# The last stage of a fused decoder kernel: rows padded to the full height, a product moved to GpSimd, gathers issued one after another

## The reference

```
y = _moe(h, ...)                 # out.at[token].add(expert_row * weight): two expert rows per token
x = _layer_norm(ALPHA * x + gate2 * y, ln_g, ln_b)
# layer_norm: (x - mean) * rsqrt(var + EPS) * g + b, over the 1024 columns
```

## Time and profile before

| | us |
|---|---|
| median of 3 runs | 2516.42 |
| lowest and highest | 2508.06, 2516.82 |
| the profiled execution | 2516.12 |
| its span, first to last instruction | 2514.5 |
| the last stage in it | about 2445 to 2514.5 |

### The profile page before, as it was taken

The page is one execution under the profiler, slowest core; times in us unless marked ns, Lnnn a source line. Parts: engine busy times, 40 slices in busy tenths (PEclk is TensorE's granted clock), DMA queues, the critical chain, the costliest instruction groups (busy, mean ns, idle before and its releaser), DMA issues. The chain is left out here.

```text
span 2514.5 us, 39237 instructions
## 1 busy us (share of the span) xinstructions
PE 2263.1 (90%) x11454; PEld 1662.9 (66%) x11454; DVE 1380.7 (55%) x2350; ACT 1075.2 (43%) x1830; POOL 307.8 (12%) x387
## 2 busy tenths in 40 slices
PE   7999997869769999999698999999989399999976
PEld 4766665648558888887486665656667288888851
DVE  4223213658866755764583344433369767755657
ACT  3211213631136645654343343444331256754645
POOL 0000002640001101010110333000000011000102
PEclk8999997979879999999899999999989699999985
DMA  7566555643248867784745644232350378866956
GB/s 276 177 214 218 204 200 154 183 163 134 71 175 295 318 224 266 284 289 154 228 154 198 195 143 151 92 96 93 101 210 35 131 282 320 318 240 220 321 198 214
DMA packets 194483, 499.26 MB, mean 199 GB/s; under 512 B 19344, under 2 KB 39281, under 8 KB 187888
## 3 DMA queue, kind: packets, MB, share of 16 engines
q1 hardware_dynamic: 164910, 403.86, 46.9%
q0 software_dynamic: 18416, 64.11, 7.2%
q10 hardware_dynamic: 11058, 30.06, 3.2%
HBM read 432.41 MB, written 68.70 MB: 199 GB/s over the span
## 5 line engine op out<-in xcount | busy, mean ns | idle before, releaser
L2024 DVE TENSOR_TENSOR e_wl<-e_raw,e_wh 128x1024 fp32r<-128x1024 f32 x384 | 451.6, 1220 | 107.9 <-ACT e_wh L1936 107.5
L1936 ACT CAST e_wh<-e_raw 128x1024 fp32r<-128x1024 f32 x384 | 379.3, 1047 | 75.8 <-DMA e_raw<-in_e_gate 22.5
L1855 PE MATMUL e_psG<-e_wh,e_xh 128*128 128x512 f32 x784 | 322.0, 411 | 10.5 <-issue 7.7
L1857 PE MATMUL e_psG<-e_wh,e_xl 128*128 128x512 f32 x784 | 312.4, 398 | 0.0
L1856 PE MATMUL e_psG<-e_wl,e_xh 128*128 128x512 f32 x784 | 310.9, 397 | 0.0
L1855 PEld LDWEIGHTS e_psG<-e_wh,e_xh 128*128 128x128 f32 x784 | 149.1, 190 | 43.2 <-issue 8.7
L1857 PEld LDWEIGHTS e_psG<-e_wh,e_xl 128*128 128x128 f32 x784 | 148.7, 190 | 37.1
L1856 PEld LDWEIGHTS e_psG<-e_wl,e_xh 128*128 128x128 f32 x784 | 149.5, 191 | 32.0
L608 PE MATMUL in_ps<-in_w_upper,in_h_upper 128*128 128x512 f32 x384 | 155.7, 405 | 3.8 <-DVE in_h_lower L328 3.4
L1855 PE MATMUL e_psY<-e_wh,e_hh 128*128 128x512 f32 x392 | 155.3, 396 | 2.8 <-DVE e_hl L2047 2.8
L1857 PE MATMUL e_psY<-e_wh,e_hl 128*128 128x512 f32 x392 | 157.1, 401 | 0.0
(11 more groups left out here) (589 smaller groups left out, 4236.7 us busy)
## 6 DMA issues: line engine op xcount, KB each, us to landing
e_raw<-in_e_gate SPq DMA_DIRECT2D x32, 2048.0 KB, 11.9
e_raw<-in_e_up SPq DMA_DIRECT2D x32, 2048.0 KB, 9.2
e_raw<-in_e_down SPq DMA_DIRECT2D x32, 2048.0 KB, 8.2
x<-in_ada_w SPq DMA_DIRECT2D x40, 1024.0 KB, 5.3
yrows<-e_y ACTq DMA_DIRECT2D x49, 512.0 KB, 7.5
x<-in_cache SPq DMA_DIRECT2D x64, 320.0 KB, 3.3
a_pages<-in_cache SPq DMA_DIRECT2D x64, 320.0 KB, 3.5
qkvo<-in_out SPq DMA_DIRECT2D x48, 256.0 KB
```

The source lines that it names most:

```text
L1855: T.matmul(out, upper[:, k, :], wh[:, z, cols], start=k == 0, stop=False)
L1857: mm = T.matmul(out, lower[:, k, :], wh[:, z, cols], start=False, stop=k == PIECES * n - 1)
L1936: S.copy(wh[:, z, c * PC:(c + 1) * PC], raw[:, z, c * PC:(c + 1) * PC]).then_inc(s_hi[z], 1)
L2024: V.tensor_tensor(wl[:, z, at], raw[:, z, at], wh[:, z, at].bitcast(F32), ALU.subtract).then_inc(s_lo[z], 1)
```

## The change

Three edits, all in `stage_combine`:

1. The ones matrix, the two shift rows and their source have 128 rows instead of 33; the added rows are zeros in the shift rows.
2. `gated(t)` runs on GpSimd. It waits for `both(t)` and counts up a new semaphore `s_gated`, for which `residual(t)` waits. On VectorE `both(1)` now comes after `residual(0)`.
3. GpSimd issues tile 0's gathers, waits until they have landed, issues tile 1's, does `gated(0)`, waits until tile 1's have landed, and issues those of tiles 2, 3 and 4. Then it does `gated(t)` for t from 1 on, each followed by the gathers of tile t + 4.

```diff
-        lb33, both_rows, ones = sb("lb33", [33, D]), sb("lb_rows", [33, D], F32R), sb("ones33", [33, P], F32R)
+        lb33, both_rows, ones = sb("lb33", [P, D]), sb("lb_rows", [P, D], F32R), sb("ones_copy", [P, P], F32R)
+        s_gated = sem("gated")
...
-            for t in range(RING):
+            def gated(t):
+                n, z = rows_of(t), zr[0:rows_of(t), t % RING, :]
+                if t == PT:
+                    po.wait_ge(s_gateS, 16 * BATCHES)
+                elif t == 0:
+                    po.wait_ge(s_gate, 16)
+                nc.gpsimd.tensor_tensor(z, z, gate[0:n, t // PT, :], ALU.mult).then_inc(s_gated, 1)
+
+            gather(0)
+            po.wait_ge(s_g[0], 32)
+            gather(1)
+            po.wait_ge(s_both, 1)
+            gated(0)
+            po.wait_ge(s_g[1], 32)
+            for t in range(2, RING + 1):
                 gather(t)
-            for t in range(RING, TILES):
-                po.wait_ge(s_both, t - RING + 1)
-                gather(t)
+            for t in range(1, TILES):
+                po.wait_ge(s_both, t + 1)
+                gated(t)
+                if t + RING < TILES:
+                    gather(t + RING)
...
-            S.copy(ones[:], g.ones[0:33, :])
+            S.copy(ones[:], g.ones[:])
...
-            def gated(t):
-                n, z = rows_of(t), zr[0:rows_of(t), t % RING, :]
-                if t == PT:
-                    v.wait_ge(s_gateS, 16 * BATCHES)
-                else:
-                    v.wait_ge(s_gate, 16)
-                v.drain()
-                V.tensor_tensor(z, z, gate[0:n, t // PT, :], ALU.mult)
-
             def residual(t):
                 n, par, z = rows_of(t), t % 2, zr[0:rows_of(t), t % RING, :]
-                v.drain()
+                v.wait_ge(s_gated, t + 1)
                 V.scalar_tensor_tensor(out=z, in0=g.x[0:n, t, :], scalar=ALPHA, in1=z, op0=ALU.mult, op1=ALU.add,
                                        accum_out=total[0:n, par:par + 1])
...
             both(0)
-            gated(0)
-            both(1)
             for t in range(TILES):
                 residual(t)
-                if t + 1 < TILES:
-                    gated(t + 1)
                 if t == 0:
+                    both(1)
                     v.wait_ge(s_lg, 16)
                 centred(t)
                 reciprocal(t)
```

## The result

| | before | after |
|---|---|---|
| median, us | 2514.89 (10 runs) | 2521.27 (10 runs) |
| lowest to highest | 2508.06 to 2519.05 | 2515.95 to 2528.86 |
| ratio | | 1.0033, 95% interval 1.0022 to 1.0044 |
| span of the profiled execution | 2514.5 | 2514.1 |
| first gather of the last stage starts at | 2446.44 | 2438.38 |

The two spans are nearly equal, and that misleads: the program ahead of the last stage, which the change does not touch, happened to be 8.06 us shorter in this execution. The last stage is 7.66 us longer, which agrees with the ratio (0.33% of 2514.89 is 8.3 us). A second profile of the changed kernel (e8) shows how well this measure repeats.

The account below looks back on a forecast made before the run. VectorE and TensorE share one pace; exclusion makes VectorE the bound. `residual(1)` 2472.0, four tiles of 6.3, two of 6.05, then TensorE's last tile, copy and end give span 2525.4, so 2527.0 us; range 2515 to 2533.

Parts of the forecast that it names:

- rival B: TensorE's clock released at the end: last tile at 2.4 GHz, minus 2.7 us, 2524.3; chance 0.20.
- D: No exclusion at this size and a low clock: TensorE bounds again from near 2469.5, giving 2520; chance 0.10.
- Exclusion: GpSimd's product (2.36 us) and VectorE's `residual`, `centred`, `both`, all reading two SBUF tiles, cannot overlap; their times add.
- The pace: Between `residual` starts: 6.3 us in tiles with gathers, 6.05 without, both above TensorE's 5.45.
- Without exclusion: Pace would be 4.8 us a tile, since the reciprocal waits for ScalarE's deviation, 3.16 us after `residual` starts.
- Who goes first: After `both`, VectorE's `residual` wins over GpSimd's next product, as it starts 0.1 us after `both`.
- C: GpSimd's product goes first, `residual` waits 2.2 us, 6.95 us per tile, 2532, slower; chance 0.20.
- Tile 0: Its gathers alone land at 2452.5 (2453.7 at worst, as now); `residual(0)` at 2458.5, 0.7 us gained.
- Tile 2: Second gather held by `both(1)`, so rows land at 2466.6, not 2461.2; ScalarE's square of tile 0 waits behind `first(2)`.
- Padding: 128 rows for the ones matmul: no instruction added, could release TensorE's clock, but the forecast keeps it low.
- Descriptor issues: On GpSimd, a gather's issue is held by a two-input VectorE instruction: 1.97 us against 0.94 alone; otherwise near 2525.

Follow-up runs that it names:

- e8: The changed kernel profiled a second time, nothing changed; stage 75.75 us against 75.72, span 2524.8 against 2514.1.
- e5: e2 with GpSimd zeroing a scratch tile after a drain in place of each gate product, so the gate is left out; stage 92.68 us.
- e7: e2 with ScalarE writing `first(t)` into PSUM, so `both` reads one operand there; stage 68.82 us against 70.58.
- e9: Kernel before plus padding, tile 3's gathers held back, `first` in PSUM, VectorE reordered, products of tiles 5 to 8 on GpSimd; ratio 0.9984, stage 62.06 us.
- e1: Kernel before with the padding to 128 rows alone; stage 65.05 us against 68.06.
- e4: Changed kernel with 33 rows again instead of 128; stage 79.55 us against 75.72.
- e2: Changed kernel with the gathers of tiles 0 to 3 issued at once again; stage 70.58 us against 75.72.

## Why the prediction was right, and where it was not

- *Outcome.* Forecast 2527.0 with 2515 to 2533, no change at 0.5%; measured 2521.27. What happened is nearest to rival B (2524.3), to which I gave half the chance of the forecast. In the stage's own time the forecast was 78.96 us and the measured one is 75.72: 1.6 us of the difference are there at R7 (62.86 against 61.29), 1.5 are the last tile (5.45 against 3.92). The class, no change, says little for the mechanism: the forecast, B and D all give it.
- *Exclusion.* Right, and the row that carried it was a small one: 0.17 us grown to 1.86 beside a product. e5 and e7 confirm the two sides of it. The product's duration, 2.36 us by interpolation, is 2.35 where nothing holds it.
- *The pace.* I summed 6.3 us for four intervals and 6.05 for two; they are 6.82 once and 5.67 to 5.71 otherwise, R1 to R7 35.3 against 37.3. Two terms were wrong. I charged `both`, its drain and the next `residual` 1.37 us from start to start, but the change takes the drain out: 1.19 (2492.81 to 2494.00). And I let the product come behind `centred` in tiles with gathers; it came before the work of `centred` every time, once after a start so late that the interval grew to 6.82. Without exclusion I had 4.8, by the chain through ScalarE's deviation; e5 and e9 show 4.46.
- *Who goes first.* VectorE, as assumed: 1.21 us for `residual` in the tile shown, the product held. C did not occur in the changed kernel, for the reason I had given, the small advantage of VectorE (2488.31 against 2488.46). It did occur once in e7, where the product did not have to wait for `both`.
- *Tile 0.* I let it land 1.2 us sooner by itself and expected R0 at 12.06. `first(0)` starts at 7.07 against 7.29, and R0 is 12.75 against 12.76. Over all profiles it starts at 6.51 to 7.07 with the gathers one by one and at 7.03 to 7.40 with three or four tiles' queued at once: the queued gathers of other tiles cost tile 0 about half a microsecond, and this part of the change had no more than that to win.
- *Tile 2.* Direction and mechanism right (each wait, then an issue held by `both`, and ScalarE's `first(2)` ahead of the square), size short: expected at 20.2, it came at 22.0. The failing term is the 4.4 us from issue to landing; for tile 0 it was 5.8 us from the start of the second issue to ScalarE's start (2439.62 to 2445.45), and from the end of the hold to ScalarE's start 5.0 us for tile 1 (2447.79 to 2452.79) and 5.3 for tile 2 (2455.13 to 2460.41). R1 at 25.56 was close to 26.03 all the same, because in my sum it hung on the product of tile 1, behind the issues of tiles 3 and 4. I had that end at 24.3 and it ended at 25.0; in the trace `both(2)` starts at 24.8, when the reciprocal behind `first(2)` and the square is there and that product is about to end.
- *Padding.* I held it for open and took the low clock. The rows of the kernel before had the evidence, 128-row matmuls that rose and a mixture with 64 rows that did not the earlier trace rows; I weighed it too low, on the thought that an idle TensorE would not hold the clock. e1 and e4 refute the conclusion, and the thought is half right: of the nine five-microsecond windows of after from 2465 on, five are at 0.92 to 1.00, but three are at 0.71 to 0.73, where the clock fell back. The Trainium skill ("TensorE: Matmul & The Clock Gate", Part 1) says that the clock is set "based on how busy the PE has been recently". These runs show that this is not all: TensorE is busy 5.00 of 5 us at 0.50 with 33 rows, and 1.77 of 5 us at 1.00 with 128.
- *What the clock is worth.* B said 2.7 us, half of the last tile; after against e4 is 3.8, before against e1 3.0. In the last tile itself it is 1.6 us (5.53 to 3.92), since most of that tile ran at 0.50, and more than half of this 1.6 comes with the rows at either clock (4.64 in e2). The rest of the 3.8 is that in e4 R7 is 1.05 us later and TensorE starts its last tile 6.2 us after it and not 5.1. For low clock I had written a stage of 78.96 (2525.4 less 2446.44), and e4 has 79.55, but that closeness is an accident: the pace was 2 us too high, and I had missed that TensorE, started late (at 30.42, where rival D has a start at 23.1, since the diagonal also waits for `first(3)`), becomes the bound.
- *Descriptor issues.* The page "SBUF — State Buffer", Who interferes with whom, of the Trainium skill takes them not to be held by a `tensor_tensor` with both inputs in SBUF, and calls this inferred. The traces disagree: 1.97 us in before and 1.78 in e2 beside that instruction, and in after 1.80 and 1.74 us beside `both`, against 0.94 alone. But an issue in before that began 0.01 us after `both(0)` (2454.92 against 2454.91) took 0.94 us, so not every overlap holds it.

## What to carry to other kernels

When an instruction moves from VectorE to GpSimd, ask first which of its neighbours in VectorE's list read two operands from SBUF: with those it takes turns, at GpSimd's 2.35 us instead of VectorE's 1.22, and only an instruction with one operand in PSUM, placed beside it on purpose, gives something back (4.46 against 5.69 us a tile). Waiting for one transfer before the next is issued pays the whole latency once per wait, and pays it for whatever is queued behind the last of them. And when a change touches 3% of a long program, measure that stage from its own first instruction: the stage gave 75.72 and 75.75 us where the whole differed by 10.7. Even so, its parts moved by up to 0.8 us, so ask for a second profile before a difference of half a microsecond is read. Where TensorE ends the stage, a small matmul is worth padding to the full number of rows: here it cost no instruction and made TensorE's tile 0.9 us shorter at the low clock and 3.1 us at the high one.

## What the runs showed of the hardware that I had not expected

- The number of rows of a small matmul decided whether TensorE's clock rose: with 33 rows in one of three passes it stayed at 1.2 GHz for over 40 us of unbroken work; with 128 rows, 95 of them zeros against ones, it was at 2.4 GHz 2.9 to 6.1 us after the start.
- It did not stay there. In after it fell back to 1.2 GHz for about 3 us three times, with gaps of up to 3.2 us in TensorE's work; e2 shows two falls of about 10 us (at 0.50 from 2472 to 2482 and from 2489 to 2499) and a third under the whole last tile. How much of the last tile it hits no edit controlled: that tile took 2.45, 3.92 and 4.64 us in e7, after and e2.
- At the same clock of 1.2 GHz a half with 33 rows takes 2.73 us and one with 128 rows 2.13.
- A VectorE instruction is not held by a GpSimd memset that only writes (1.22, 1.28 and 2.23 us beside each other in e5), nor if one of its operands is in PSUM (1.26 and 2.37 us in e7).
- A drain on GpSimd after two gathers' issues left it idle 4.7 us in e5, about the time from a gather's issue to its landing; that it waits for the landing is argued from this number, not shown.
